# Attention sub-layers: the order of slabs, steps, weight splits and the first out-projection pieces

## The reference, cut to what matters

```
mp = adaln(c_ctx[None, :], w_ada[li], b_ada[li])       # silu(cond) @ w + b, split in 9
h = modulate(rmsnorm(x, g_pre), shift, scale)
q, k, v = split(h @ w_qkv, [1024, 1280], axis=-1)      # 16 heads of 64, 4 key/value heads
# latent tokens: rope on q and k, a window of 128 in the latent keys, plus 128 cached keys
s = einsum('bnqkgd,bnskd->bnkgqs', qb, kb) * ATTN_SCALE
p = softmax(concatenate([s_lat, s_ctx, sink], axis=-1))
o = p[..., :n_band] @ vb + p[..., n_band:-1] @ v_ctx
x = x + gate * rmsnorm(o.reshape(B, L, 1024) @ w_o, g_post)
```

## Time and profile before

| | us |
| --- | --- |
| median of 3 runs | 3286.37 |
| lowest and highest run | 3283.35, 3288.7 |
| the profiled execution's own time | 3282.8 |
| its span | 3280.9 |
| TensorE busy in it | 3083.7 (94%) |
| attention sub-layer 1: first product to first scores, then heads | 83.8, 70.3 |
| attention sub-layer 10: the same | 67.2, 70.4 |

### The profile page before, as it was taken

One profiled execution on the slowest core, in us unless ns is written; L12 is line 12 of the kernel. 1 busy time (PEld: TensorE's weight loads), 2 busy tenths in 40 slices (PEclk: granted clock), 3 DMA queues, 4 the chain that ended last, 5 costly groups with the idle time before them and its releaser, 6 DMA issues. The chain is left out here.

```text
span 3280.9 us, 48857 instructions
## 1 busy us (share of the span) xinstructions
PE 3083.7 (94%) x19610; PEld 2836.7 (86%) x19610; DVE 2155.5 (66%) x2879; ACT 1139.0 (35%) x1941; POOL 575.8 (18%) x578
## 2 busy tenths in 40 slices
PE   6999879999999999999999997679999999979999
PEld 5999758999899998998999997468998999868998
DVE  4777486777776657776876535647777877585444
ACT  3222454223422424223322433234224222454222
POOL 1112101112111111112111102642112112201001
PEclk8999999999999999999999998679999999999999
DMA  7666414666565446665665443024664766313443
GB/s 267 199 206 185 146 43 134 198 217 190 184 196 173 115 123 192 193 211 168 206 205 149 128 127 98 15 68 156 216 201 148 225 203 204 112 43 95 126 127 97
DMA packets 565510, 515.80 MB, mean 157 GB/s; under 512 B 42965, under 2 KB 499238, under 8 KB 563494
## 3 DMA queue, kind: packets, MB, share of 16 engines
q1 hardware_dynamic: 565286, 512.68, 51.0%
HBM read 509.37 MB, written 3.24 MB: 156 GB/s over the span
## 5 line engine op out<-in xcount | busy, mean ns | idle before, releaser
L1342 PE MATMUL bank<-h_hi,w_hi 128*128 128x384 f32 x3328 | 1116.8, 336 | 3.8 <-DVE tmp L1801 3.8
L1344 PE MATMUL bank<-h_hi,w_lo 128*128 128x384 f32 x3328 | 1114.8, 335 | 0.0
L1343 PE MATMUL bank<-h_lo,w_hi 128*128 128x384 f32 x3328 | 1114.2, 335 | 0.0
L1757 DVE TENSOR_TENSOR w_lo<-raw,w_hi 128x1024 fp32r<-128x1024 f32 x648 | 804.1, 1267 | 411.8 <-ACT w_hi L1603 406.9
L1603 ACT ACTIVATE w_hi<-raw 128x1024 fp32r<-128x1024 f32 x648 | 679.1, 1059 | 1015.7 <-PE bank L1375 483.8
L1779 DVE SCALAR_TENSOR_TENSOR fold<-ada_raw,cond,fold 128x1024 f32<-128x1024 f32 x462 | 638.5, 1438 | 0.0
L1342 PEld LDWEIGHTS bank<-h_hi,w_hi 128*128 128x128 f32 x3328 | 625.6, 188 | 12.9 <-DVE tmp L1801 6.0
L1343 PEld LDWEIGHTS bank<-h_lo,w_hi 128*128 128x128 f32 x3328 | 625.5, 188 | 5.8
L1344 PEld LDWEIGHTS bank<-h_hi,w_lo 128*128 128x128 f32 x3328 | 625.3, 188 | 0.0
L2069 POOL TENSOR_TENSOR h_lo<-tmp,h_hi 128x384 fp32r<-128x384 f32 x176 | 284.9, 1619 | 1786.5 <-DVE h_hi L1805 1786.5
L1371 PE MATMUL bank<-w_hi,h_hi 128*128 128x512 f32 x1056 | 334.4, 398 | 0.0
(11 more groups left out here) (200 smaller groups left out, 2512.0 us busy)
## 6 DMA issues: line engine op xcount, KB each, us to landing
raw<-w_ffn_in SPq DMA_DIRECT2D x352, 512.0 KB, 5.0
ada_raw<-w_ada SPq DMA_DIRECT2D x272, 512.0 KB, 4.2
raw<-w_ffn_out SPq DMA_DIRECT2D x176, 512.0 KB, 4.8
raw<-w_hgrn_in SPq DMA_DIRECT2D x40, 512.0 KB, 4.7
g_rows<-g_dram SPq DMA_DIRECT2D x12, 1024.0 KB, 6.8
raw<-w_attn_qkv SPq DMA_DIRECT2D x24, 512.0 KB, 5.3
raw<-w_conv_in SPq DMA_DIRECT2D x24, 512.0 KB, 4.9
ada_first<-w_ada SPq DMA_DIRECT2D x16, 512.0 KB, 10.6
```

Of the source, the lines that this page charges most:

```text
L1342: mm(out, wh, h_hi[:, k, :], start=(k == 0), stop=False)
L1343: mm(out, wh, h_lo[:, k, :], start=False, stop=False)
L1344: last = mm(out, wl, h_hi[:, k, :], start=False, stop=(k == DC - 1))
L1757: V.tensor_tensor(w_lo[:, b % RING, :], raw[:, b % RAW, :], w_hi[:, b % RING, :].bitcast(F32), ALU.subtract).then_inc(w_lo_made, 1)
```

## The change

- Slabs of sub-layer 1: SyncE issues one behind each of input blocks 2 to 5, and one behind each of blocks 13 to 16. TensorE's first half stays behind block 2, the second goes from block 4 to block 9. The attention constants are issued behind block 10 instead of 5.
- Steps: turn behind block 6 (was 5), keys in two portions behind 7 and 8, two rotations each behind 9, 10 and 11, and the last two behind the scores of the first pair. A step waits for the copy of the block before (`evacuated(p - 1)`). The turns use four banks.
- ScalarE and VectorE work block by block instead of in pairs; the splits of blocks 16 and 17 go behind the heads.
- Behind the last two rotations TensorE does ten products that nobody reads.
- VectorE copies the bank of 384 columns of the turned probabilities, ScalarE the one of 512.
- Token tiles 0 and 1 of the out-projection of chunks 0, 1 and 2 stand among the last heads, tile 2 behind the loop.
- GpSimd makes the next sub-layer's `s_cols` behind its rotations instead of ahead of them.

```diff
+BEHIND = 4
+DRAIN = 3
...
-    MIX_GAPS = {"attn": [2, 4], "conv": [], "hgrn": []}
+    MIX_GAPS = {"attn": [2, 9], "conv": [], "hgrn": []}
...
         def turn_probs(h):
             n = HEADS * a + h
             pe.wait_ge(p_normed, n + 1)
-            if h == 0:
-
-                pe.wait_ge(rope_sin, ROPE * (a + 1))
-            else:
+            if h > 0:
                 pe.wait_ge(pt_copied_v, n)
                 pe.wait_ge(pt_copied_a, n)
...
         for j in range(DC + 2):
             if j < DC:
                 scores(j)
+            if j == 0:
+                for r in range(*ROPE_LATE):
+                    pe_rotate(pe, s, r)
+                pe.wait_ge(mods_made, units_end[s])
+                for _ in range(10):
+                    mm(psum[5][:, 0:P], ident, ones[:, :], start=True, stop=True)
+            if j == DC:
+
+                pe.wait_ge(score_read, HEADS * (a + 1))
+                out_part(0, range(2))
             if 1 <= j <= DC:
                 turn_probs(2 * j - 2)
+            if j == DC:
+                out_part(1, range(2))
             if j >= 2:
+                if j == DC + 1:
+                    out_part(2, range(2))
                 values(j - 2)
             if 1 <= j <= DC:
                 turn_probs(2 * j - 1)

+        pe.wait_ge(pt_copied_v, HEADS * (a + 1))
+        pe.wait_ge(pt_copied_a, HEADS * (a + 1))
+        for c in range(DRAIN):
+            out_part(c, range(2, NT))
...
-    ATTN_STEPS = {5: "turn", 7: "keys", 9: (4, 8), 11: (8, 12)}
+    ATTN_STEPS = {6: ("turn",), 7: ("keys", 0, 2), 8: ("keys", 2, 4), 9: ("queries", 4, 6), 10: ("queries", 6, 8),
+                  11: ("queries", 8, 10)}
+    ROPE_LATE = (10, 12)
...
-        evacuated(p)
-        if step == "turn":
+        evacuated(p - 1)
+        if step[0] == "turn":
             pe.wait_ge(attn_in, 16 * 5 * (a + 1))
+
+            pe.wait_ge(rows_copied, units_end[s])
...
-                if n >= 2:
-                    pe.wait_ge(attn_turn_copied, 5 * a + n - 1)
+                if n >= 4:
+                    pe.wait_ge(attn_turn_copied, 5 * a + n - 3)
                 for q, src in enumerate(srcs):
-                    last = nc.tensor.transpose(psum[4 + n % 2][:, q * P:(q + 1) * P], src, ident)
+                    last = nc.tensor.transpose(psum[4 + n % 4][:, q * P:(q + 1) * P], src, ident)
...
-            A(pt[h % 3][:, 512:KEYS], psum[5][:, 0:KEYS - 512], ACT.Copy).then_inc(pt_copied_a, 1)
+            A(pt[h % 3][:, 0:512], psum[4][:, :], ACT.Copy).then_inc(pt_copied_a, 1)
...
-            V.tensor_copy(pt[h % 3][:, 0:512], psum[4][:, :]).then_inc(pt_copied_v, 1)
+            V.tensor_copy(pt[h % 3][:, 512:KEYS], psum[5][:, 0:KEYS - 512]).then_inc(pt_copied_v, 1)
...
                 maxima(2 * j + 1)
+                if j == 0:
+                    for r in range(*ROPE_LATE):
+                        dve_rope(dve, s, r)
                 normalize(2 * j)
...
-                        slabs.setdefault(p + 4 + n // 2, []).append((half // 2, half % 2 * (DC // 2) + n))
+                        slabs.setdefault(p + (4 if half % 2 else 0) + n, []).append((half // 2, half % 2 * (DC // 2) + n))
...
-                elif b == (5 if sub_kind[s] == "attn" else in_blocks[s] - 1):
+                elif b == (10 if sub_kind[s] == "attn" else in_blocks[s] - 1):
                     sp_core_start(sp, s)
...
                     else:
                         pe.wait_ge(rows_copied, half // 2 + 1)
-                    ada_half(half, 6, slab_landed(half))
-            pe_core(pe, s)
+                        pe.wait_ge(k_dup_copied, KVH * (attn_number(s) + 1))
+                    ada_half(half, 4 if half % 2 else 6, slab_landed(half))
+            pe_core(pe, s, lambda c, tiles: out_block(s, c, b0 + n_in + c, tiles=tiles))
...
+                    if ph.kind == "qkv":
+                        for j in range(4):
+                            p = 4 * i + j
+                            dve_attn_step(dve, s, p)
+                            if p in gaps and gaps[p] % 2 == 1:
+                                ada_add(gaps[p], 4)
+                            if p in turns:
+                                mod_add(turns[p], 5)
+                            if p + 6 < n_in + BEHIND:
+                                split(b0 + p + 6)
+                        continue
...
             dve_core(dve, s)
-            for c in range(DC - TAIL):
-                split(b0 + n_in + c + 6)
+            for c in range(BEHIND if sub_kind[s] == "attn" else 6, DC - TAIL + 6):
+                split(b0 + n_in + c)
```

More of the change, by code:

```diff
@@ L605, in pe_attn_step @@
         else:
-            for r in range(*step):
+            for r in range(*step[1:]):
                 pe_rotate(pe, s, r)
@@ L611, in act_attn_step @@
         a = attn_number(s)
-        step = ATTN_STEPS.get(p)
-        if step == "turn":
+        step = ATTN_STEPS.get(p, ("none",))
+        if step[0] == "turn":
             for n in range(5):
@@ L642, in act_mix @@
         block = ph.block0 + 4 * i
-        if ph.kind == "qkv":
-            for j in (ja, jb):
-                act.wait_ge(block_done, block + j + 1)
-                A(qkv[:, qkv_chunk(4 * i + j), :], psum[j][:, 0:T], ACT.Copy).then_inc(bank_free[j], 1)
-        elif ph.kind == "conv_z":
+        if ph.kind == "conv_z":
             act.wait_ge(block_done, block + ja + 1)
@@ L1390, in out_ready, with out_block @@
                 pe.wait_ge(o_lo_made, DC * mixer_number(s) + c + 1 + CREDIT)
-        def out_block(s, c, b, between=None):
+        def out_block(s, c, b, between=None, tiles=range(NT)):
             pe.wait_ge(w_lo_made, b + 1)
@@ L1396, in out_block @@
             hi, lo = moving_out(s, c)
-            for t in range(NT):
+            for t in tiles:
                 last = out_tile(b, t, hi, lo, c == 0, False)
@@ L1400, in out_block @@
                     between()
-            last.then_inc(block_done, 1)
+            if t == NT - 1:
+                last.then_inc(block_done, 1)
         def turn_normed(e, t):
@@ L1547, in mixer @@
                     pe.wait_ge(st_copied[z], PAIRS + 1)
-            for c in range(DC - TAIL):
+            for c in range(DRAIN if sub_kind[s] == "attn" else 0, DC - TAIL):
                 out_block(s, c, b0 + n_in + c)
@@ L1822, in mixer @@
                         p = ph.block0 - b0 + 4 * i + 2 * half
-                        for q in (p, p + 1):
-                            if q in gaps and gaps[q] % 2 == 1:
-                                ada_add(gaps[q], 6)
-                            if q in turns:
-                                mod_add(turns[q], 7)
-                        if ph.kind == "qkv":
-                            dve_attn_step(dve, s, p + 1)
                         split(b0 + p + 6)
@@ L2077, in mixer @@
                     gp_mix(gp, ph, i)
-            if sub_kind[s] != "conv":
+            if sub_kind[s] == "hgrn":
                 gains(s)
+            elif sub_kind[s] == "attn":
+                out_gains(s)
             gp_core(gp, s)
+            if sub_kind[s] == "attn":
+                scale_gains(s + 1)
         gp.sem_inc(o_lo_made, CREDIT)
```

59 lines of the change are left out of this document (32 added, 27 removed).

## The result

The changed kernel takes 3242.8 us (median of 4 runs, 3241.64 to 3243.08), the kernel before 3285.2 in the same series (4 runs, 3283.35 to 3288.7). The ratio is 0.987, with a 95% interval of 0.986 to 0.988: 42.4 us less, where the prediction said 3243.7 and 42.7. (The 3286.4 of the prediction is the median of the first three runs of the kernel before; a fourth, with the same program, brought it to 3285.2.) The profiled execution has a span of 3241.2 us in place of 3280.9.

What follows compares the result with a forecast made beforehand. TensorE, busy 94% of the span, was taken as the bound, its idle or slow-clock stretches in attention as the gain. Savings of 27.3 (sub-layer 1) and 15.4 (sub-layer 10), together 42.7 us, gave 3243.7, eight-in-ten range 3234 to 3258.

Steps and rivals of the forecast that it cites:

- Slabs, 11.9: Sub-layer 1, behind block 2 of the projection: earlier slabs remove TensorE's wait and its lower clock, saving 11.9 us.
- Attention steps, 6.8 a layer: Projection steps wait only for the copy of the block before: transposes 0.9, keys 0.7, queries 5.2 us saved, range 5 to 8.
- Start of the heads, 1.9: First scores: two splits moved behind the loop let VectorE read scores sooner, saving 1.9 us a layer, range 1 to 2.3.
- Ten unread products: Behind the first scores: they stand in TensorE's 5.52 us idle stretch ahead of the second pair's scores and cost 0.
- rival 3: Next FFN starts late because its first blocks' splits and loads come after the loop, some 5 us a layer: 3254; chance 0.07.
- Copies, 1.9 a layer: Head loop: VectorE copying 384 columns instead of 512 saves 0.136 us on each of fourteen copies, 1.9 a layer (0 to 2.5).
- VectorE is what counts: Head loop, 449 to 487.8: VectorE, busy 37.3 of 38.8 us, is what the loop waits for, with TensorE at 28.8.
- End of the loop, 4.8 a layer: Out-projection pieces among the last heads fill TensorE's idle time, saving 4.8 us a layer, range 3 to 5.5.
- all terms at their high ends: Whole kernel with every saving at the top of its range: 3236 us.
- 1: Slabs or constants still late, SyncE held or transfers crowding each other; costs sub-layer 1's 11.9 us: 3255.6; chance 0.07.
- 2: Head loop takes as long as before: ScalarE's copy becomes the wait, pieces only push the last transposes: 3257; chance 0.11.
- 4: TensorE's clock stays lower from the loop's end through the out-projection, 32.7 us more a layer: 3309; chance 0.03.

Runs made afterwards that it cites:

- slabs_back: Changed kernel with sub-layer 1's slabs issued behind blocks 6 and 7 and attention constants behind block 5 again: 73.36 us to sub-layer 1's first scores, against 63.04.
- before_slabs: Kernel before with only the slab order changed, each half's four slabs behind four blocks in a row: ratio 0.999 (0.998 to 1.000), median 2.9 us lower.
- no_filler: Changed kernel without the ten unread products behind the first scores of each attention sub-layer: median 3240.5 us.
- pieces_back: Changed kernel with the out-projection of the first three chunks whole behind the last values again: median 11.9 us higher, 9.0 of it in the attention sub-layers.

## Why the prediction was right, point by point

- **Slabs, 11.9.** 10.3 by slabs_back, and mechanism and place are right. What the text held wrong is whose gain it is. It costed the second half's move at nothing, and before_slabs shows that the order of the slabs alone is worth 3.6. The two sub-layers differ in their gain by 28.45 - 16.33 = 12.1, nearer still to the 11.9 than the 10.3 of slabs_back, which keeps the second half at block 9.
- **Attention steps, 6.8 a layer.** First product to scores is 8.5 shorter in sub-layer 10, where there are no slabs, above the range of 5 to 8. All three terms were too small. From product to product around the steps, less one spacing, the transposes went from 3.00 to 1.43 us (1.6 saved, 0.9 taken), the keys from 5.25 to 3.92 (1.3 for 0.7), the queries from 8.4 to 2.39 (6.0 for 5.2), 8.9 together, of which 0.4 is given back between the steps. I took 0.2 of idle for each switch and it is nothing, TensorE being busy for 58.62 of 58.64 us; that is 0.6 of the 1.7 missed. The rest is that the steps' own products go faster without waits between them than I took from rows that had waits.
- **Start of the heads, 1.9.** The first pair takes 5.43 to 5.44 in place of 7.32 (first scores to second), which is 1.9, with the maxima at 1.95 and 2.10. But it was put down to the splits, and putting them back costs 0.6 a layer. The late rotations, costed at nothing, cost about 1.4 here and give 3.4 ahead of the scores, 0.78 of it the wait for the block's own copy.
- **Ten unread products.** Taken as 0. In the attention sub-layers that is right; in the whole kernel it is wrong, no_filler is 2.3 us faster (rival 3).
- **Copies, 1.9 a layer.** Mis-sized: 0.4 and 0.8. The step that failed is "VectorE is what counts": it was busy for 37.3 of 38.8 us, so a wait was near, and 0.19 of the saved 0.27 a pair went into it.
- **End of the loop, 4.8 a layer.** The two lines of the first table around the last values give, in sub-layer 10, 17.63 + 42.93 before and 20.82 + 34.80 after: 4.9. pieces_back gives 4.3 and 4.7. Right.
- **The terms of a layer together.** 1.7 too little for the steps, 0.1 too little for the end and 0.9 too much for the heads' start and the copies (3.8 taken, 2.9 between the first scores of pair 1 and pair 8) make 16.3 where 15.4 was said: in part luck. In the range, all terms at their high ends give 3237.9 by the prediction's own numbers, not 3236.
- **Rivals.** 1 and 2 didn't come (2 did in a small part: the copies). 4 didn't: the granted clock is 1.00 in the 14.86 us of pieces, values and two sets of transposes, and in the out-projection behind. The Trainium skill, in "TensorE: Matmul & The Clock Gate", Part 4, says that transposes don't count as activity for the clock in the way that other products do. No run tests that, since none had transposes alone there; with other products between them the clock stayed up.
- **Rival 3 and the 5.1 us lost elsewhere.** The sub-layer after the attention starts in time: last values to its first product take 34.80, which is 42.94 less the 8.1 of the pieces. The loss is further on. In sub-layers 2 to 9 TensorE waits longer for VectorE's `tmp`, before and after:

```profile
PE bank L1342 <- DVE tmp L1801: 3.1, 6, 0.6
```

```profile
PE bank L1373 <- DVE tmp L1839: 6.0, 6, 1.5
```

VectorE waits there in its turn for ScalarE, and that for a `raw<-w_ffn_in` tile. This is ScalarE in sub-layer 2 of the kernel before, the changed kernel and no_filler, 10.4, 11.4 and 10.8 us behind the sub-layer's first product:

```profile
551.69 1.06 ACT L1603 ACTIVATE w_hi<-raw 128x1024 fp32r<-128x1024 f32 x1 [2.58 <-DMA raw<-w_ffn_in]
```

```profile
525.34 1.06 ACT L1636 ACTIVATE w_hi<-raw 128x1024 fp32r<-128x1024 f32 x1 [3.60 <-DMA raw<-w_ffn_in]
```

```profile
523.82 1.06 ACT L1634 ACTIVATE w_hi<-raw 128x1024 fp32r<-128x1024 f32 x1 [3.02 <-DMA raw<-w_ffn_in]
```

The load is issued at the same place in all, 6.6 us behind the first product, and lands later. In the changed kernel one transfer of 16 KB stands between issue and landing, in a queue that the profile calls "instruction"; I take it for a load of an engine's code:

```profile
q8 instruction: 1, 0.02, 1.6%
```

That is the DMA view from 520.5 to 524.3. The same stretch of the kernel before and of no_filler has no such line. In us behind the sub-layer's first product (code transfer, landing of the load) and TensorE's wait for `tmp`:

```
                 sub-layer 2           sub-layer 8           sub-layer 11
before           12.0  10.35  0.42     none  10.52  0.56     none  10.62  0.69
before_slabs     11.0  10.54  0.61     none  10.42  0.50     none  10.31  0.36
after             7.6  11.38  1.46      7.7  11.44  1.53      8.1  11.53  1.61
no_filler        12.4  10.79  0.86     11.3  10.65  0.76     none  10.64  0.71
```

("none": none in the first 12.5 us.) The ten other kernels made from the changed one all have a code transfer at 7.6 to 9.3 in these three sub-layers. Over all 14 traces and seven feed-forward sub-layers, this load lands at 11.07 to 12.30 in the 33 cases with a code transfer beside it, and at 10.24 to 11.04 in the 65 without. Against the kernel before, sub-layers 2, 8 and 11 are 1.03, 0.95 and 0.93 us longer, 2.9 of the 5.1. no_filler differs from the changed kernel in TensorE's stream alone, and its transfers come 3.6 to 4.8 us later in sub-layers 2 and 8 and miss the load; in sub-layer 11 there is none. So what stands earlier in a stream decides where the code transfer falls. That the code is TensorE's is likely, but the profile doesn't name the engine, and how such a transfer delays the load isn't shown.

Another 1.15 us are in sub-layer 0, ahead of everything that was changed, and come from one execution to the next: among the kernels made from the changed one, alike up to there, its length is 292.5 to 293.9 us. The last 1.0 is spread over the others in parts of 0.4 at most. The total came out as predicted by luck, because three things met: the terms were 2.1 us too small together, 5.1 were lost elsewhere, and the profile of before lay 2.4 under its median.

All single undoings add up to 35.9 of the 44.8 us. The rest, some 9, must be in what wasn't undone alone (the second half's move, the smaller portions on alternate banks) and in what the parts give each other; no run divides it.

## What to carry to other kernels

A wait that is taken away early in a chain can bring out the next one, as 8 of 12 us did here: see what each later consumer then finds, and move its loads or its place in the same edit. In a loop where one engine is busy for over 95%, unloading it by some tenths of a microsecond a turn gives only what the next ring has to spare; draw that ring from starts and releasers, operation by operation, before you size the term. An engine's idle stretch at a loop's end is best filled with ready work of the next stage, which pays twice when it also keeps TensorE's clock up. Unread products that raise the clock where another engine sets the pace bring nothing, and instructions that look free can move a load of code onto a transfer that the next stage waits for: compare the sub-layers that weren't touched too.

## What was not expected of the hardware

- A code transfer of 16 KB beside a 512 KB load of weights puts its landing off by some 0.9 us (11.5 for 10.6 us behind the sub-layer's first product, the middle values of 33 and 65 cases). Ten products more in TensorE's stream at sub-layer 1 were enough to bring this about in sub-layers 2 and 8.
- VectorE's add of a rotation took 0.93 us at 408.50 and 0.42 at 409.87, the same instruction on the same shape. During the first GpSimd worked on its own two rotation products:

```profile
407.74 1.41 POOL L856 TENSOR_TENSOR qkv<-qkv,attn_k 128x256 f32<-128x256 f32 x2 [3.60 <-PE bank L599]
```

  During the second it was idle. Over both layers of the changed kernel, the six adds of query rotations that started while GpSimd worked took 0.93 to 0.94 us, the ten others 0.42 to 0.43. In the kernel before four of twelve took 0.43 beside GpSimd, so it is not every overlap.
- TensorE's eight slab products took 0.64 us at the full clock and 1.08 at the lower one. A wait alone doesn't lower it: in before_slabs they took 0.64 behind 1.99 us of idle and 1.08 behind 2.41 more. In slabs_back waits of 7.1 us cost 10.3 in this way.
- SyncE's issues of equal 512 KB loads took between 0.37 and 2.49 us in before_slabs from 359 to 366 us; what it depends on wasn't looked into.
